# Retention's splits behind its chains, a third score ahead, squares by halves, the row behind retention in another buffer, and the second chunk one norm tile later

## The chip, the cores and the metric

The kernel runs on one core of a Trainium2 chip. The metric is the device time of one execution in microseconds (us), the median of several runs; lower is better. TensorE is called PE in the profile, its weight loads PEld, VectorE DVE, ScalarE ACT, GpSimd POOL, SyncE SP.

## What is computed

Two layers (DEPTH 2) of a diffusion trunk with D_MODEL 1024 over 512 latent tokens and 256 context tokens, all in float32:

```python
h = modulate(rms_norm(x, g_mix[l]), mod[:, :, 0], mod[:, :, 1])
y, yc = token_mixer(h, hc, ...)        # retention, latent attention, grouped attention, gates, w_out
x = x + mod[:, :, 2] * y
h2 = modulate(rms_norm(x, g_ffn[l]), mod[:, :, 3], mod[:, :, 4])
x = x + mod[:, :, 5] * swiglu(h2, w_ffn_in[l], w_ffn_out[l])
```

The context stream `xc` goes through the same steps in the first layer only; in the second it gives keys and values alone. `mod` is `silu(c) @ w_mod + b_mod`. The part that matters most here is retention, four heads with keys of 128 and values of 256 channels. Per head, with q and k rotated (rope), a score is a product of k and q times a decay that falls with the distance of the tokens; the output is the sum of scores times values:

```python
scores = jnp.einsum('bnihd,bnjhd->bnhij', qc, kc) * decay
inner = jnp.einsum('bnhij,bnjhe->bnihe', scores, vc)
y = rms_norm(y).reshape(B, T, RET_W)
return (jax.nn.silu(g.astype(jnp.float32)) * y).astype(g.dtype)
```

The kernel computes the recurrence between chunks as one masked product over all tokens, with both directions' decays in one table.

## The kernel before

**Layout.** Channels lie on the 128 partitions, tokens on the free axis: 768 of them (`TOK`), latent 512 first, in layer 0; in layer 1 queries and outputs have 512 (`LAT`). A float32 product is made of three fast ones: each operand is split into a rounded part (ACT writes it, `wh`, `hh`, `qh`, `pth`, `yh`) and a rest (DVE or POOL subtracts it, `wl`, `hl`, `ql`, `ptl`, `yl`), and `three` (L1435 is its matmul) multiplies high with high, high with low, low with high.

**Weights.** All weights come in one stream of chunks of 128 x 1024. SP loads chunk after chunk into two slots of `raw`, each when the slot's last rest is written (L423 to L425). `split(at, k)` exists twice: ACT's (L431) waits for the chunk and for the product that last used the slot and writes `wh`; DVE's (L910) then writes `wl`. `project` on PE waits for `wl` and counts `product` when it is done. Every engine works its own list of instructions in order; semaphores alone tie them together. The lists are written by hand.

**Retention** (kind `ret`): for each head PE projects q (slot 0), transposes the values from `vraw` (which ACT loads a head ahead), projects k and the gate g, and then makes 8 (layer 0) or 6 (layer 1) units: a score of 128 x 512 (or 256) into one of three PSUM banks, the product with `dec` on DVE into `prob`, the rounded part on ACT into `pth`, the rest on POOL into `ptl`, and six matmuls of values on PE. ACT and DVE prepare q and k in between (copy, rope, rounded part, rest) and split the coming weights: split(2) is g's weight, split(3) the next head's q, split(4) the next head's k. At the end of a head ACT squares both halves of the output (`y_sq`), PE sums them over the channels with `ones`, ACT takes the root (`v_std`), DVE the reciprocal, and the output is scaled, gated and split into `yh`, `yl`.

**Merge** (kind `merge`) multiplies a branch's output with its output matrix, eight chunks in four turns of two, and adds them gated to `xz`. In layer 0 each merge also computes eight columns' worth of modulation: ACT loads a row of `w_mod` (`mod_load`), PE multiplies it (`mod_row`, L1548) and folds four partial sums (`mod_fold`, L1562), DVE adds the bias (L1056, `m_add`). `rows_of` gives the two buffers of the rows: `mraw`, which shares its bytes with `dec`, and a part of `prob`. The merge behind retention has `begun` 0; those behind the attentions have 6 tiles done already.

**Two chunks at once.** `pair_tile` multiplies one normalised tile of 128 channels with the chunks in both slots while the norm makes the next tile. It is used in the kernel's start, at layer 1's entry and at the start of both feed-forward parts.

## Time and profile before

| | us |
|---|---|
| median of 3 runs | 3473.76 |
| lowest, highest | 3471.82, 3473.92 |
| the profiled execution | 3469.6 |
| its span | 3467.4 |

The mean granted clock of TensorE over the span is 0.973 of full speed. The span counts from the first instruction of the program to the last; 2.2 us of the profiled execution lie outside it. A row of the timeline gives the start, how long the group of merged instructions lasted, engine, line, operation, tiles (written <- read), their count, and in brackets the idle time of the engine before it and what ended it. Ends of matmuls are modelled and overlap the start of the next.

### The profile page before, as it was taken

Reading aid. Unit: us, or ns where it says so; the run is one execution under the profiler, and the core shown is the slowest. Engines: PE = TensorE matmul, PEld = TensorE weight load, DVE = VectorE, ACT = ScalarE, POOL = GpSimd, SP = SyncE. Lnnn points to the kernel's source line nnn. Section 1 sums busy time; section 2 is a strip of 40 time slices with the busy share of each in tenths; the row PEclk is TensorE's granted clock in tenths of the full one; section 3 lists DMA queues with packets and bytes.
Section 4 is the critical chain, followed back from the end, with each engine's and each line's share of the span. In section 5 each row is a group of like instructions: output and inputs, shape, how many; then the busy total and the mean of one; then the engine's idle time right before and its main releaser. Section 6 shows DMA issues by size and latency. Waiting matters only on the chain.

```text
span 3467.4 us, 49699 instructions
## 1 busy us (share of the span) xinstructions
PE 3218.3 (93%) x18760; PEld 2733.4 (79%) x18760; DVE 1507.6 (43%) x2047; ACT 1241.1 (36%) x1777; POOL 391.3 (11%) x304
## 2 busy tenths in 40 slices
PE   6999999999998989999999988999999988799998
PEld 5788888899887777788888867887788776678886
DVE  5555523444335533422222355553455455443334
ACT  3344432444433432321211234444355533432222
POOL 0011100111102201010100101111011101010001
PEclk9999999999999999899999999999999999989999
DMA  4221132111231244123132332222222232323222
GB/s 183 74 74 67 67 122 81 62 59 61 89 129 56 67 128 139 56 80 126 62 126 85 128 117 87 75 79 88 83 70 70 94 109 67 112 79 97 95 95 101
DMA packets 100921, 315.17 MB, mean 91 GB/s; under 512 B 11088, under 2 KB 21456, under 8 KB 100816
## 3 DMA queue, kind: packets, MB, share of 16 engines
q1 hardware_dynamic: 55872, 202.40, 17.8%
q10 hardware_dynamic: 44944, 111.32, 9.7%
q8 instruction: 72, 1.18, 0.1%
q14 instruction: 33, 0.27, 0.0%
HBM read 283.79 MB, written 29.88 MB: 90 GB/s over the span
## 4 chain that ended last, share of the span: by engine, by line
PE 48%; issue 6%; DVE 3%; ACT 2%; POOL 1%; DMA 0%; ACTq 0%; DVEq 0%; POOLq 0%
PE ps L1435 45%; PE ps L1521 1%; PE ps L1548 1%; POOL ptl L1417 1%; DVE wl L913 1%; ACT wh L439 1%; DVE tmp L923 0%; DVE hl L1088 0%; PE ps L1562 0%; DVE tmp L1079 0%; ACT prob L490 0%; PE ps L1491 0%; DMA xz<-xspill 0%; PE ps L1459 0%; ACTq L672 0%
## 5 line engine op out<-in xcount | busy, mean ns | idle before, releaser
L1435 PE MATMUL ps<-hh,wh 128*128 128x512 f32 x2768 | 832.5, 361 | 41.3 <-DVE wl L913 17.6
L1435 PE MATMUL ps<-hh,wl 128*128 128x512 f32 x2768 | 813.3, 354 | 0.0
L1435 PE MATMUL ps<-hl,wh 128*128 128x512 f32 x2768 | 813.0, 354 | 0.0
L913 DVE TENSOR_TENSOR wl<-raw,wh 128x1024 fp32r<-128x1024 f32 x364 | 484.2, 1331 | 541.2 <-ACT wh L439 512.9
L1435 PEld LDWEIGHTS ps<-hh,wh 128*128 128x128 f32 x2768 | 454.8, 191 | 123.0 <-issue 40.4
L1435 PEld LDWEIGHTS ps<-hh,wl 128*128 128x128 f32 x2768 | 453.0, 190 | 75.2
L1435 PEld LDWEIGHTS ps<-hl,wh 128*128 128x128 f32 x2768 | 453.8, 190 | 73.7 <-issue 0.7
L439 ACT ACTIVATE wh<-raw 128x1024 fp32r<-128x1024 f32 x364 | 383.2, 1054 | 222.3 <-PE ps L1435 186.6
L1435 PE MATMUL ps<-yh,wh 128*128 128x512 f32 (+1 forms) x1296 | 408.3, 369 | 30.4 <-DVE wl L913 18.9
L1435 PE MATMUL ps<-yl,wh 128*128 128x512 f32 (+1 forms) x1296 | 395.7, 360 | 0.0
L1435 PE MATMUL ps<-yh,wl 128*128 128x512 f32 (+1 forms) x1296 | 395.6, 360 | 0.0
L1370 POOL TENSOR_TENSOR prob<-prob,ri 128x768 f32<-128x768 f32 x160 | 208.3, 1303 | 1448.6 <-DVE ri L953 1448.6
L1435 PEld LDWEIGHTS ps<-yh,wh 128*128 128x128 f32 x1296 | 216.1, 191 | 83.0 <-issue 36.3
L944 DVE TENSOR_REDUCE mx<-ps 128x1 f32<-128x768 f32 x160 | 135.9, 849 | 308.8 <-PE ps L1435 308.8
L1435 PEld LDWEIGHTS ps<-yh,wl 128*128 128x128 f32 x1296 | 216.5, 191 | 37.6
L1435 PEld LDWEIGHTS ps<-yl,wh 128*128 128x128 f32 x1296 | 216.4, 191 | 36.5 <-issue 0.2
L480 ACT ACTIVATE pth<-ps 128x768 fp32r<-128x768 f32 x160 | 116.1, 726 | 308.4 <-PE ps L1521 308.3
L1435 PE MATMUL ps<-pth,vh 128*128 128x256 f32 (+1 forms) x528 | 167.8, 318 | 34.6 <-POOL ptl L1417 24.0
L1424 POOL TENSOR_TENSOR yl<-prob,yh 128x768 f32 (+1 forms) x44 | 69.1, 1570 | 845.7 <-ACT yh L892 845.7
L1435 PE MATMUL ps<-ptl,vh 128*128 128x256 f32 (+1 forms) x528 | 164.2, 311 | 0.0
L1435 PE MATMUL ps<-pth,vl 128*128 128x256 f32 (+1 forms) x528 | 164.1, 311 | 0.0
L959 DVE TENSOR_TENSOR ptl<-ps,pth 128x768 fp32r<-128x768 f32 x160 | 135.2, 845 | 58.7 <-ACT pth L480 58.6
(190 smaller groups left out, 3423.4 us busy)
## 6 DMA issues: line engine op xcount, KB each, us to landing
raw<-in_stream SPq DMA_DIRECT2D x364, 512.0 KB, 3.5
mraw<-in_wmod ACTq DMA_DIRECT2D x40, 512.0 KB, 3.5
prob<-in_wmod ACTq DMA_DIRECT2D x40, 512.0 KB, 3.5
gspill<-prob ACTq DMA_DIRECT2D x32, 384.0 KB, 2.3
tmp<-gspill ACTq DMA_DIRECT2D x24, 384.0 KB, 3.2
early_y<-in_wmod SPq DMA_DIRECT2D x12, 512.0 KB, 14.1
vraw<-gspill ACTq DMA_DIRECT2D x16, 384.0 KB, 3.9
dec<-in_dec ACTq DMA_DIRECT2D x8, 768.0 KB, 4.3
```

Of the source, the lines that this page charges most:

```text
L439: act.activation(wh[:, s, :], raw[:, s, :], ACT.Copy).then_inc(sem("w_hi"), 1)
L480: act.activation(pth[:, 0:st, (m % 2) * P:(m % 2) * P + P], ps[:, TRANS:TRANS + st * P].rearrange("p (s q) -> p s q", q=P), ACT.Copy).then ...
L913: dve.tensor_tensor(wl[:, s, :], raw[:, s, :], wh[:, s, :].bitcast(F32), ALU.subtract).then_inc(sem("w_lo"), 1)
L944: dve.tensor_reduce(mx[:, n:n + 1], ps[:, s0:s0 + w], AX.X, ALU.max).then_inc(sem("s_max"), 1)
L959: dve.tensor_tensor(ptl[:, 0:st, cols], ps[:, TRANS:TRANS + st * P].rearrange("p (s q) -> p s q", q=P), pth[:, 0:st, cols].bitcast(F32), A ...
L1370: pool.tensor_tensor(prob[:, c.prob(m), 0:w], prob[:, c.prob(m), 0:w], ri[:, col:col + 1].to_broadcast([P, w]), ALU.mult).then_inc(sem("s_ ...
L1417: pool.tensor_tensor(ptl_f[:, cols], prob[:, u % 3, 0:w], pth_f[:, cols].bitcast(F32), ALU.subtract).then_inc(sem("rs_lo"), 1)
L1424: pool.tensor_tensor(yl[:, bass.ds(2 * i + k, 1), 0:nt], prob[:, k:k + 1, 0:nt], yh[:, bass.ds(2 * i + k, 1), 0:nt].bitcast(F32), ALU.subt ...
L1435: ins = pe.matmul(out, lhs[w], rhs[x](cols), start=start and n == 0, stop=stop and n == 2)
L1521: ins = pe.transpose(ps[:, TRANS + s * P:TRANS + (s + 1) * P], prob[:, c.prob(m), s * P:(s + 1) * P], ident[:, :])
L1548: return pe.matmul(ps[r0:r0 + STRIP, col:col + P], csil[:, kt, :], x, start=kt < NSTRIP, stop=kt >= KT - NSTRIP)
```

## The change

Eight edits, all in the order of work and in one buffer:

- ACT's split(4) and the Silu of the gate's other half move from ahead of the units to behind the third rounding; DVE's split(3) moves from ahead of k's rope to behind it, and its split(4) behind the fourth decay product.
- PE issues three scores ahead instead of two.
- A new semaphore `y_half` tells ACT that the first half of the output is complete; the first square waits for it alone, and PE sums each half as soon as it is squared.
- The wait for `m_add` in `ret` moves behind the q projection, in `gqa_in` behind the first two projections.
- The merge behind retention takes its even rows from `vraw` instead of `mraw`, and ACT asks for the first row in the last head, behind the transposes of the values.
- PE waits for `v_std` before that merge's first `mod_row`, since the row's sums share a bank with retention's sums.
- `pair_tile` multiplies the second chunk one tile behind the first; the last call does both remaining tiles.

```diff
@@ plan
-             "y_sq": 2, "v_full": 2, "v_hi": 2, "v_lo": 2}, ROPED, ROPED, VALUES)
+             "y_sq": 2, "y_half": 1, "v_full": 2, "v_hi": 2, "v_lo": 2}, ROPED, ROPED, VALUES)
-        if ph["kind"].endswith("_last"):
+        if ph["kind"].endswith("_last") or ph["kind"] == "ret":
             ph["merge"] = after
@@ rows_of
-            return mraw[:, :], prob_f[:, x0:x0 + CH]
+            return vraw_f[:, 0:CH] if ph["kind"] == "merge" and not ph["begun"] else mraw[:, :], prob_f[:, x0:x0 + CH]
@@ ACT, merge
-                    if ph["nmod"]:
+                    if ph["nmod"] and ph["begun"]:
                         mod_load(ph, 0, ph["j0"])
@@ ACT, ret
                         if not last:
                             load_values(8 * i + (ph["g0"] + 4 * h + 4))
+                        elif ph["merge"]["nmod"]:
+                            mod_load(ph["merge"], 0, ph["merge"]["j0"])
...
                         act.activation(tmp[:, 1, 0:nt], pair(0)[:, 0:nt], ACT.Silu).then_inc(sem("free0"), 1)
-                        if not last:
-                            split(t, 4)
-                        act.wait_ge(sem("rg_in"), t.v("rg_in", 1) * 16)
-                        act.activation(tmp[:, 2, 0:nt], tmp[:, 2, 0:nt], ACT.Silu)
...
                             act.activation(pth_f[:, (u % 3) * LAT:(u % 3) * LAT + w], prob[:, u % 3, 0:w],
                                            ACT.Copy).then_inc(sem("rs_hi"), 1)
-                        act.wait_ge(sem("rs_used"), t.v("rs_used", units))
+                            if u == 2:
+                                act.wait_ge(sem("rg_in"), t.v("rg_in", 1) * 16)
+                                act.activation(tmp[:, 2, 0:nt], tmp[:, 2, 0:nt], ACT.Silu)
+                                if not last:
+                                    split(t, 4)
                         for e in range(2):
+                            if e == 0:
+                                act.wait_ge(sem("y_half"), t.v("y_half", 1))
+                            else:
+                                act.wait_ge(sem("rs_used"), t.v("rs_used", units))
@@ DVE, ret
-                        split(t, 3)
                         roped(t, (1, 1), 1, 1, 1, kh, kl, 0, TOK)
-                        if not last:
-                            split(t, 4)
+                        split(t, 3)
...
                                               dec[:, d0:d0 + w], ALU.mult).then_inc(sem("rs_sd"), 1)
+                            if u == 3 and not last:
+                                split(t, 4)
@@ PE, pair_tile
-                for slot in range(2):
+                for slot, g in ((0, kt), (1, kt - 1)) + (((1, kt),) if kt == KT - 1 else ()):
+                    if g < 0:
+                        continue
@@ PE, gqa_in
-                    pe.wait_ge(sem("m_add"), at.v("m_add"))
...
                         pe.wait_ge(sem("free0"), at.v("free0", j + 1))
+                        if j == 0:
+                            pe.wait_ge(sem("m_add"), at.v("m_add"))
@@ PE, merge
                                 elif ph["nmod"]:
+                                    if late and not k + r:
+                                        pe.wait_ge(sem("v_std"), at.v("v_std"))
                                     mod_fold(t, k) if r else mod_row(t, k, ph)
@@ PE, ret
-                    pe.wait_ge(sem("m_add"), at.v("m_add"))
...
                         pe.wait_ge(sem("v_std"), t.v("v_std"))
+                        pe.wait_ge(sem("m_add"), at.v("m_add"))
...
                         score(1)
+                        score(2)
...
-                            if u + 2 < units:
-                                score(u + 2)
+                            if u + 3 < units:
+                                score(u + 3)
...
+                                if e == 0 and u == units - 1:
+                                    ins.then_inc(sem("y_half"), 1)
                             ins.then_inc(sem("rs_used"), 1)
-                        pe.wait_ge(sem("y_sq"), t.v("y_sq", 2))
-                        for r0, r1 in ranges(nt):
-                            for e, x in enumerate((tmp[:, 0, r0:r1], prob[:, 2, r0:r1])):
-                                ins = pe.matmul(pair(AUX)[:, r0:r1], ones[:, :], x, start=e == 0, stop=e == 1)
+                        for e, x in enumerate((tmp[:, 0, :], prob[:, 2, :])):
+                            pe.wait_ge(sem("y_sq"), t.v("y_sq", e + 1))
+                            for r0, r1 in ranges(nt):
+                                ins = pe.matmul(pair(AUX)[:, r0:r1], ones[:, :], x[:, r0:r1], start=e == 0, stop=e == 1)
```

## Rows read from the trace of the kernel before

**Rows 1.** The page: busy time and share of the span by engine.

```profile
PE 3218.3 (93%) x18760; PEld 2733.4 (79%) x18760; DVE 1507.6 (43%) x2047; ACT 1241.1 (36%) x1777; POOL 391.3 (11%) x304
```

**Rows 2.** PE's waits, 1014 to 1231 us: releaser, total us, times, longest.

```profile
PE ps L1435 <- POOL ptl L1417: 12.5, 4, 3.7
PE ps L1819 <- ACT prob L822: 6.4, 4, 1.6
```

**Rows 3.** PE's waits, 2796 to 2975 us, layer 1's retention.

```profile
PE ps L1435 <- POOL ptl L1417: 11.4, 4, 3.3
PE ps L1435 <- DVE kl L933: 9.6, 4, 2.4
PE ps L1819 <- ACT prob L822: 4.7, 4, 1.2
```

**Rows 4.** Timeline, layer 0: first head's sums, second head's start of the units.

```profile
1065.04 1.12 PE L1819 MATMUL ps<-tmp,ones 128*128 128x512 f32 x2 [1.60 <-ACT prob L822]
...
1096.31 1.23 DVE L913 TENSOR_TENSOR wl<-raw,wh 128x1024 fp32r<-128x1024 f32 x1 [2.48 <-ACT wh L439]
1098.88 3.73 POOL L1417 TENSOR_TENSOR ptl<-prob,pth 128x512 fp32r<-128x512 f32 x3 [36.54 <-ACT pth L818]
1100.20 0.80 PE L1435 MATMUL ps<-pth,vh 128*128 128x512 f32 x1 [3.67 <-POOL ptl L1417]
```

**Rows 5.** Timeline, layer 0, last head: first product of the values.

```profile
1200.19 0.50 PE L1435 MATMUL ps<-pth,vh 128*128 128x512 f32 x1 [1.50 <-POOL ptl L1417]
```

**Rows 6.** Windows: length, busy us of PE, PEld, DVE, ACT, POOL; PEclk, DMA share, GB/s.

```profile
1100.20:1103.60 3.40, 3.40 (x8) 2.73 (x9) 0.00 (x0) 0.00 (x0) 2.41 (x2) 0.50 0.08 34
1200.20:1203.60 3.40, 3.40 (x15) 2.83 (x16) 0.69 (x1) 0.32 (x1) 2.42 (x2) 1.00 0.00 0
...
1015.40:1018.80 3.40, 3.35 (x11) 2.90 (x12) 0.97 (x1) 0.00 (x0) 0.00 (x0) 0.57 0.87 310
1231.30:1236.80 5.50, 5.49 (x30) 4.40 (x31) 1.03 (x1) 2.08 (x3) 0.00 (x0) 0.50 0.80 270
1424.50:1427.90 3.40, 3.40 (x13) 2.92 (x12) 1.96 (x1) 1.41 (x2) 1.82 (x1) 0.50 0.44 145
```

**Rows 7.** Timeline, layer 1, second head: k's copy, split(3), scores, values.

```profile
2851.68 0.81 ACT L456 ACTIVATE tmp<-ps 128x768 f32<-128x768 f32 x1 [2.09 <-PE ps L1435]
2853.47 1.23 DVE L913 TENSOR_TENSOR wl<-raw,wh 128x1024 fp32r<-128x1024 f32 x1 [1.42 <-ACT wh L439]
2859.52 0.50 PE L1435 MATMUL ps<-qh,kh 128*128 128x512 f32 x1 [2.43 <-DVE kl L933]
2865.18 0.80 PE L1435 MATMUL ps<-pth,vh 128*128 128x512 f32 x1 [3.33 <-POOL ptl L1417]
```

**Rows 8.** Timeline: first projections of `gqa_in` and of retention in layer 0.

```profile
548.29 0.61 PE L1435 MATMUL ps<-hh,wh 128*128 128x512 f32 x2 [1.18 <-DVE mods L1056]
1015.45 1.00 PE L1435 MATMUL ps<-hh,wh 128*128 128x512 f32 x2 [2.82 <-DVE mods L1056]
```

**Rows 9.** Timeline, layer 0: last head's rests, first row and fold of the merge.

```profile
1225.22 1.83 DVE L1283 TENSOR_TENSOR yl<-prob,yh 128x768 fp32r<-128x768 f32 x2
1231.31 1.08 PE L1548 MATMUL ps<-mraw,csil 128*32 128x128 f32 x16 [9.82 <-DMA mraw<-in_wmod]
1233.14 0.26 ACT L598 ACTIVATE tmp<-ps 128x128 f32<-128x128 f32 x1
1238.64 0.28 PE L1562 MATMUL ps<-sel,tmp 128*128 128x2 f32 x2
```

**Rows 10.** Timeline: the kernel's start, and the third chunk of both feed-forward parts.

```profile
39.38 0.16 DVE L1119 TENSOR_TENSOR mods<-ps,bmod 128x4 f32<-128x4 f32 x1 [2.31 <-PE ps L1667]
1423.36 0.59 PE L1435 MATMUL ps<-hh,wh 128*128 128x512 f32 x2 [2.15 <-DVE wl L913]
3100.56 0.77 PE L1435 MATMUL ps<-hh,wh 128*128 128x512 f32 x1 [2.30 <-DVE wl L913]
```

**Rows 11.** One line's view, L913: count, ns minimum/median/maximum, first and last start.

```profile
L913 DVE TENSOR_TENSOR wl<-raw,wh x364: 1215/1226/2156, 18.2 to 3447.2; 128x1024 fp32r<-128x1024 f32 x182
```

More of the change, by code:

```diff
@@ L332, in build @@
         prob_f = prob[:, :, :].rearrange("p a b -> p (a b)")
+        vraw_f = vraw[:, :, :].rearrange("p a b -> p (a b)")
         def rows_of(ph):
             x0 = 2 * TOK if ph["kind"] == "merge" else 0
-            return mraw[:, :], prob_f[:, x0:x0 + CH]
+            return vraw_f[:, 0:CH] if ph["kind"] == "merge" and not ph["begun"] else mraw[:, :], prob_f[:, x0:x0 + CH]
         keys, queries = ((kh, kl), (k2h, k2l)), ((qh, ql), (q2h, q2l))
@@ L1252, in turn @@
                                           ALU.subtract).then_inc(sem("vt_lo"), 1)
+                        roped(t, (1, 1), 1, 1, 1, kh, kl, 0, TOK)
                         split(t, 3)
-                        roped(t, (1, 1), 1, 1, 1, kh, kl, 0, TOK)
-                        if not last:
-                            split(t, 4)
                         units = 8 if nt > LAT else 6
@@ L1464, in pair_tile @@
                 pe.wait_ge(sem("n_lo"), at.v("n_lo", kt + 1 + since))
-                for slot in range(2):
+                for slot, g in ((0, kt), (1, kt - 1)) + (((1, kt),) if kt == KT - 1 else ()):
+                    if g < 0:
+                        continue
                     s = at.slot(slot)
                     outs = [(pair(slot)[:, r0:r1], (r0, r1)) for r0, r1 in ranges(nt)]
-                    ins = three(outs, [w[:, s, whole(kt)] for w in (wh, wl)],
-                                [lambda c, x=x: x(kt, c) for x in H], kt == 0, kt == KT - 1)
-                    if kt == KT - 1:
+                    ins = three(outs, [w[:, s, whole(g)] for w in (wh, wl)],
+                                [lambda c, x=x: x(g, c) for x in H], g == 0, g == KT - 1)
+                    if g == KT - 1:
                         ins.then_inc(sem("product"), 1)
```

## The prediction

> **What bounds the kernel now.** I read the page first: TensorE is busy for 93% of the span and no other engine for half of it [rows 1], so time comes back only where TensorE waits or runs slowly. Then I listed TensorE's waits over the two retention stages and looked at each in the timeline. In layer 0 the four heads hold 12.5 us of waits for POOL's `ptl` and 6.4 us for ACT's squares [rows 2]; in layer 1 they hold 11.4 us for `ptl`, 9.6 us for DVE's `kl` and 4.7 us for the squares [rows 3]. Around them lie single waits: 1.18 and 2.82 us for the last sum of the modulation (`mods`) [rows 8], and 9.82 us for a row of w_mod, the longest behind the kernel's first [rows 9]. Last comes the clock: in 3.4 us TensorE starts 15 matmuls of 512 columns at full clock (0.227 us each) and 8 at half of it [rows 6]. So a long wait is paid again behind its end: 15 matmuls' worth of time gives 8, and 3.4 us at half clock cost up to 1.7 us, 1.6 with the matmuls counted (8 x 0.2).
>
> **Splits behind the chains.** TensorE's first values product needs score, decay product (DVE), rounding (ACT) and rest (POOL). In the heads before the last one DVE makes the split of the next k weight first, 1.23 us from 1096.31 [rows 4], behind ACT's part of it; the first product of the values starts at 1100.20 after 3.67 us idle [rows 4]. The last head has no such split: there the wait is 1.50 us, with the same three scores before it [rows 5]. That is what the change makes of the others: 3.67 - 1.50 = 2.17 us a head in layer 0. The clock stands at 0.50 behind the 3.67 us and at 1.00 behind the 1.50 us [rows 6], so 1.6 us more. The split itself is not free: on ACT the gate's Silu (0.8 us for a pass over 768 columns [rows 7]) and the split (1024 columns, so 1.1 us) now stand between the third and fourth rounding, on DVE 1.23 us between the fourth and fifth decay product. Behind the first values product TensorE needs 9 x 0.227 = 2.05 us a unit (one score, two values), the chain of a unit only what POOL needs, 3.73 us for three, 1.25 each [rows 4]; stepping the chain through with the durations of this case I find each later rest ready 0.4 to 2 us before TensorE asks. I take nothing for it. Bounds: nothing, and 1 us a head if that cover is short.
>
> **Splits and the shared queue.** The L913 rows last 1.22 us in the middle and up to 2.16 us [rows 11]; the split now runs beside POOL's `ptl`, where a long one is possible. It would use up 0.9 us of a cover of 0.4 to 2 us. The Trainium skill ("SBUF — State Buffer", section "Who interferes with whom") says that a VectorE tensor_tensor with both inputs in SBUF and a GpSimd instruction that reads SBUF exclude one another for a whole instruction. By that rule each of six heads could give back up to 1 us, 6 us in all; the rows' spread agrees with it, their middle does not show it. The sum goes without it.
>
> **Third score.** It was already issued before the first wait; now the fourth is too, 3 x 0.227 = 0.68 us of TensorE work that fills part of the 1.50 us left. Its bank is freed by the first decay product, which ends before the third score does. 0.68 us a head, eight heads.
>
> **k's rope ahead of split(3).** In layer 1 the scores wait 2.43 us for `kl` [rows 7]. DVE idled 1.42 us until ACT's part of split(3), then split for 1.23 us until 2854.7, then began k's rope [rows 7]; k's copy had been there since 2852.5 (2851.68 + 0.81) [rows 7]. The rope can start then: 2.1 us earlier, with 0.3 us of wait left. All four heads of layer 1 show this wait (9.6 us in four) [rows 3]. In layer 0 nothing waits for `kl` and I count nothing. split(3) then ends about when the first score does; it may hold the first decay product by 0.1 us. It is wanted a whole head later, and the reload of its raw buffer, which SyncE's queue issues behind it, with it.
>
> **Layer 1's chain** shows 3.33 us before the values product [rows 7]; three such and one of 1.48 make the 11.4 us [rows 3]. So 3.33 - 1.48 = 1.85 us less 0.1 for split(3), plus 1.6 us of clock, in three heads.
>
> **Squares by halves.** The first square starts when the last unit's first half is done, 3 matmuls of 256 columns (0.36 us) earlier in layer 0 and 3 of 512 (0.68 us) in layer 1, and the sums over it start at once; the second square (0.8 us) lies beside them, as even the first two matmuls of the sums take 1.12 us [rows 4]. The wait of 1.60 us (6.4 in four) [rows 2] falls to about 0.5, that of 1.18 (4.7 in four) [rows 3] to 0.1: 1.1 us a head, eight heads.
>
> **Heads, summed.** Layer 0: 3 x (2.17 + 1.6 + 0.68 + 1.1) + (0.68 + 1.1) = 18.4 us. Layer 1: 3 x (2.1 + 1.75 + 1.6 + 0.68 + 1.1) + (2.1 - 0.1 + 0.68 + 1.1) = 21.7 + 3.8 = 25.5 us. Behind a head's sums the order of root, reciprocal, products and `yl` is as before, so nothing of this is taken back before the next head's transposes.
>
> **m_add later.** The two waits of 1.18 and 2.82 us [rows 8] stood before a projection that doesn't need them; their semaphore comes 1.2 and 2.9 us after TensorE is ready, and the projections take 8 us or more. Behind the 2.82 us the clock is 0.57 on the mean for 3.4 us [rows 6], so up to 1.6 us more; I take 1.5. 1.2 + 2.8 + 1.5 = 5.5 us. The k weight's split isn't wanted until 9 us later.
>
> **Row behind retention.** Now the row's transfer is issued only after the last `yl` (1225.22 to 1227.05), since `mraw` shares its bytes with `dec`; TensorE idles from 1221.5 to 1231.31 [rows 9] and runs at 0.50 until 1236.8 [rows 6]. With the row in `vraw`, loaded a head earlier, its product runs at 1221.5, two tiles follow, and the last two wait for `yl` until 1227.1. They end at about 1228.4. What is late next is the fold: it needs ACT's copy of the row's sums, which stands on ACT behind the wait for `yl`, a split, two table loads and a Sigmoid and starts at 1233.14 [rows 9]. The fold thus moves from 1238.64 [rows 9] to 1233.4: 5.2 us. TensorE idles 4.7 us before it, so the tiles behind run at half clock for one stretch, 1.6 us back. I take 3.6; bounds 2.0 (two stretches) and 5.2 (none). The added wait for v_std holds nothing: the root is over three tiles before.
>
> **Second chunk a norm later.** The first chunk's product now ends a tile earlier against the same total (a tile: 3 x (512 + 256) columns, 1.0 us, or 0.7 us at 512). Where TensorE works without idling from the first norm on and then waits for the next weight's `wl` (2.15 us at 1423.36, 2.30 us at 3100.56) [rows 10], the wait shrinks by that: 1.0 and 0.7 us. Behind the first of them the clock was 0.50 [rows 6], behind the second a matmul took 0.77 us [rows 10]; with 1.1 and 1.6 us left, which elsewhere did not lower it, 1.6 us each. In the kernel's start one tile fewer stands before the third fold, where DVE idles 2.31 us [rows 10]; behind that both engines are without idle, so I take half, 1.1 (0 to 2). At layer 1's entry the norm sets the pace and ACT's split covers the later tile: 0. Sum 1.0 + 0.7 + 3.2 + 1.1 = 6.0 us.
>
> **Sum.** 18.4 + 25.5 + 5.5 + 3.6 + 6.0 = 59.0 us. The profiled execution took 3469.6 us (span 3467.4); it would be 3410.6. The median of the runs is 4.2 us above it: 3473.8 - 59.0 = 3414.8 us.
>
> **Rivals.** (1) The clock is not given back: shorter waits, but more of them in a row (about 1 us before the values, 0.5 before the sums) still lower it in the heads and at the norms. Against it speaks the last head's 1.00 behind 1.50 us [rows 6]; for it, that half clock stood behind a wait of only 2.15 us. The sum loses 6 x 1.6 + 1.5 + 3.2 = 14.3 us: 3429 us. (2) The cover inside the chain is short, 1 to 2 us a head in six heads, and the fold behind retention stays where it was: 6 to 12 + 3.6 us, 3424 to 3430 us. (3) The change doesn't do what it says: split(4) in the middle of the chain makes the fourth unit late by what it took off the first, so only k's rope, the squares and the single waits remain: 59.0 - 3 x (2.17 + 1.75) - 6 x 1.6 - 8 x 0.68 = 32 us, 3442 us. (4) Slower: ACT's split(4) waits on raw data or on the g product while the roundings 4 to 8 stand behind it in ACT's order, and DVE's part holds decay products 5 to 8; TensorE idles once a head in mid-chain. It needs more than 59 us over six heads, about 10 us a head, to end above 3474 us; at 12 us a head it ends at 3487. From a wait of 2 us on it costs anything. Against it: the raw chunk is asked for behind the split of the g weight, a whole product (8 us) before the scores, and the g product is over when they start.
>
> **How the numbers follow.** Forecast 58%: 3408 to 3421. Rivals 1 and 2 together 25%, rival 3 8%, rival 4 3%, more gain than summed (clock kept behind retention too, start in full) 6%, to 3405. The range is 3404 to 3434. About 0.2% (7 us) is what a measurement can tell from no change: faster 0.95, same 0.02, slower 0.03.
>
> **What would show it.** Right: waits for `ptl` of about 1 us in all eight heads, none over 0.5 us for `kl`, under 0.6 us for squares, full clock in retention, no wait for `mods`, and a wait for ACT's `tmp` of over 3 us at the first fold behind retention instead of one for `mraw`. Wrong: a wait for `ptl` in mid-chain, half clock behind waits near 1 us, a longer wait before layer 1's first norm tiles.

## The result, and the profile after

The changed kernel takes 3413.4 us (median of four runs, 3408.3 to 3424.5) beside 3473.8 us before (four runs, 3471.8 to 3476.9) on the same chip: ratio 0.9831, 95% interval 0.9817 to 0.9845, so faster by 1.7%. Forecast were 3414.8 us and a ratio of 0.983. Measured again beside other runs of the kernel before it took 3413.7 us, ratio 0.9827 (0.9814 to 0.9841). One execution of e1 below took 3879 us at a mean granted clock of 0.78, where every other one lies at 0.97 or above; it is left out there. The profiled execution took 3408.35 us, span 3406.2: 61.2 us less than the span before.

The page after, span and busy time by engine, to be read against [rows 1]:

```profile
span 3406.2 us, 49718 instructions
PE 3200.3 (94%) x18760; PEld 2716.6 (80%) x18760; DVE 1512.8 (44%) x2047; ACT 1241.8 (36%) x1777; POOL 397.4 (12%) x304
```

TensorE's instructions are the same in number and 18 us shorter in sum, which is clock and not work (36.1 us less at half clock, by the figures below, are 18 us of work); the other 43 us are idle time that is gone. DVE and POOL are busy for 5 and 6 us more: that is the split lying beside POOL, below.

The waits of TensorE after, layer 0's retention (1005 to 1210 us), against [rows 2] (engine, line, releaser: total us, times, longest):

```profile
PE ps L1572 <- ACT tmp L600: 4.3, 1, 4.3
PE ps L1443 <- POOL ptl L1425: 3.3, 4, 0.8
PE ps L1835 <- ACT tmp L830: 2.2, 4, 0.5
PE ps L1443 <- DVE yl L1291: 1.9, 1, 1.9
```

and layer 1's (2757 to 2915 us), against [rows 3]:

```profile
PE ps L1443 <- POOL ptl L1425: 3.2, 4, 0.8
PE ps L1443 <- DVE yl L1291: 2.2, 1, 2.2
PE ps L1443 <- DVE kl L941: 1.3, 4, 0.3
```

The 12.5 and 11.4 us for `ptl` are 3.3 and 3.2, the 9.6 us for `kl` are 1.3, the squares' 6.4 us are 2.2, and in layer 1 they left the list. The wait for a row of w_mod, 9.82 us in [rows 9], is gone, and the fold's wait for ACT's `tmp` stands in its place, as a new line.

The timeline after, TensorE: second head's first values product, the rest of the merge's first tiles, the fold, and the two third chunks of the feed-forward parts, against [rows 4], [rows 9] and [rows 10] (start, length, instruction, tiles, in brackets the idle time ahead of it and what ended it):

```profile
1080.48 0.50 PE L1443 MATMUL ps<-pth,vh 128*128 128x512 f32 x1 [0.81 <-POOL ptl L1425]
...
1195.67 0.63 PE L1443 MATMUL ps<-yh,wh 128*128 128x512 f32 x2 [1.86 <-DVE yl L1291]
...
1202.40 0.59 PE L1572 MATMUL ps<-sel,tmp 128*128 128x2 f32 x2 [4.34 <-ACT tmp L600]
...
1390.51 0.59 PE L1443 MATMUL ps<-hh,wh 128*128 128x512 f32 x2 [1.12 <-DVE wl L921]
...
3040.95 0.47 PE L1443 MATMUL ps<-hh,wh 128*128 128x512 f32 x1 [1.63 <-DVE wl L921]
```

Windows after, behind four of these, against [rows 6] (length, busy us of PE, PEld, DVE, ACT and POOL, PEclk, DMA share, GB/s):

```profile
1080.50:1083.90 3.40, 3.40 (x15) 2.78 (x16) 2.48 (x2) 2.21 (x3) 3.38 (x3) 1.00 0.00 0
1202.40:1208.30 5.90, 5.90 (x19) 5.13 (x20) 3.16 (x4) 1.74 (x2) 0.00 (x0) 0.50 0.78 263
1390.50:1393.90 3.40, 3.39 (x19) 2.98 (x20) 1.54 (x2) 1.79 (x2) 1.58 (x1) 1.00 0.50 152
3041.00:3044.40 3.40, 3.40 (x15) 2.81 (x16) 1.75 (x2) 1.58 (x2) 1.29 (x1) 1.00 0.47 154
```

In the head's units 15 matmuls now lie in 3.4 us where 8 did. Over the whole span the granted clock stands at its lower level (1.2 GHz) for 189.5 us before and 153.4 after.

**Where the 61.2 us lie**, between events that both traces have (the start of the n-th split of a weight on DVE, or the last sums of a head):

| stretch | forecast us | measured us |
|---|---|---|
| kernel's start, third fold | 1.1 | 1.7 |
| latent attention (no edit in it) | 0 | 5.0 |
| layer 0: `m_add` at the grouped attention | 1.2 | 1.0 |
| layer 0: `m_add` at retention and the four heads | 2.8 + 1.5 + 18.4 | 22.8 |
| layer 0: row and fold behind retention | 3.6 | 2.9 |
| layer 0: out projection | 0 | -1.5 |
| layer 0: feed-forward pair | 1.0 + 1.6 | 2.0 |
| pace of the two feed-forward loops | 0 | -3.9 |
| layer 1: entry | 0 | 1.7 |
| layer 1: the four heads | 25.5 | 27.1 |
| layer 1: feed-forward pair | 0.7 + 1.6 | 2.4 |
| sum | 59.0 | 61.2 |

Of the heads, one in layer 0 takes 45.5 us instead of 51.1, one in layer 1 36.7 instead of 44.3 (start of `dec`'s transfer to the next head's). A head's gain can be taken apart from its waits. In layer 0 TensorE idled 3.67 + 1.60 = 5.3 us in a head and now idles 0.81 + 0.54 = 1.35, which is 3.9 us; the 3.4 us at half clock behind the long wait are gone too, which is 1.7. In layer 1 it idled 2.43 + 3.33 + 1.18 = 6.9 us and now 0.34 + 0.81 = 1.15, so 5.8 us, and 1.7 of clock again. That makes 5.6 and 7.5 us, beside the 5.6 and 7.6 measured.

The 1.7 us at layer 1's entry belong, in all likelihood, to the change as well. The norm there is one that `pair_tile` works beside. TensorE, before and after, and what stood behind the wait:

```profile
2045.76 1.19 PE L1491 MATMUL ps<-prob,ones 128*128 128x512 f32 x1 [2.48 <-ACT prob L691]
2015.73 0.67 PE L1501 MATMUL ps<-prob,ones 128*128 128x512 f32 x1 [1.81 <-ACT prob L693]
```

```profile
2045.80:2049.20 3.40, 3.40 (x5) 1.44 (x5) 0.10 (x1) 0.00 (x0) 0.00 (x0) 0.51 0.51 152
2015.80:2019.20 3.40, 3.40 (x14) 2.21 (x15) 0.83 (x2) 0.69 (x1) 0.00 (x0) 1.00 0.47 151
```

The wait is 1.8 us in all eleven traces with the second chunk a tile later, with the clock at 1.00 behind it in every one. It is 2.5 us in the three with both chunks together (before, e6 and e8), and the clock fell behind it in two of them.

### The profile page after: what moved, and what is told of

Same layout as the page of the kernel before. It is cut to its first block, busy times and chain, and to the rows that moved or that the text cites. A ratio compares the mean times of both kernels' runs of the same rounds, so it can differ in the third digit from the quotient of the medians.

```text
span 3406.2 us, 49718 instructions
## 1 busy us (share of the span) xinstructions
PE 3200.3 (94%) x18760; PEld 2716.6 (80%) x18760; DVE 1512.8 (44%) x2047; ACT 1241.8 (36%) x1777; POOL 397.4 (12%) x304
## 3 DMA queue, kind: packets, MB, share of 16 engines
q8 instruction: 72, 1.18, 0.1%
## 4 chain that ended last, share of the span: by engine, by line
PE 52%; DVE 4%; issue 3%; ACT 2%; POOL 0%; DMA 0%; ACTq 0%; DVEq 0%; POOLq 0%
PE ps L1443 49%; PE ps L1531 1%; PE ps L1558 1%; DVE wl L921 1%; ACT wh L441 0%; POOL ptl L1425 0%; DVE tmp L931 0%; DVE hl L1096 0%; PE ps L1572 0%; DVE tmp L1087 0%; DMA xz<-xspill 0%; PE ps L1467 0%; ACT prob L492 0%; ACTq L674 0%; PE ps L1501 0%
```

## The experiments

The yardstick is the changed kernel, 3413.4 and 3413.7 us. Its own runs lie up to 16 us apart, and so do those of its variants, so a median of four decides a term of 5 us only roughly. Each experiment was therefore also read by the length of a head (first `ptl` to first `ptl`) and by the wait that it was made for. Intervals are those of the ratio to the kernel before, taken on the same chip in turns. The experiments ran on three chips, where the kernel before took 3475.1, 3474.5 and 3471.6 us; only the last one, that of e9 to e11, also timed the changed kernel. Read by the ratios instead of the medians a difference moves by up to 3 us (e3 5.9 instead of 8.8, e6 3.5 instead of 6.6, e10 5 instead of 8.0), and only e11's interval lies clear of the changed kernel's own. So the medians say which way an edit works, and its size rests on the heads and the waits.

**The splits back ahead of the chains (e1).** In retention, on ACT and DVE:

```diff
@@ ACT, ret, ahead of the units
+                        if not last:
+                            split(t, 4)
+                        act.wait_ge(sem("rg_in"), t.v("rg_in", 1) * 16)
+                        act.activation(tmp[:, 2, 0:nt], tmp[:, 2, 0:nt], ACT.Silu)
@@ in the units, u == 2
-                                act.wait_ge(sem("rg_in"), ...); Silu; split(t, 4)
@@ DVE, ret
                         split(t, 3)
+                        if not last:
+                            split(t, 4)
@@ in the units, u == 3
-                                split(t, 4)
```

> The changed kernel with split(4) and the gate's second Silu put back ahead of the units, on ACT and DVE; all else as changed. Theory A (the first values product waits for what stands ahead of the chain, and a wait near 3 us lowers the clock): in six heads the wait for ptl is 3.67 - 0.68 = 3.0 us in layer 0 and 3.33 - 0.68 = 2.7 us in layer 1 instead of 0.8, the clock behind it is 0.50, and the kernel is 6 x 2.0 + 6 x 1.6 = 21 to 22 us slower than the changed one. Theory B (the clock falls only behind 3.3 us and more): same waits, clock 1.00, 12 us slower. Theory C (split(4) costs the same in mid-chain): no difference.

Measured: 3430.2 us (three runs, 3424.3 to 3439.8), ratio 0.9874 (0.9841 to 0.9907), 16.6 us over the yardstick. A head of layer 0 takes 49.2 us twice and then 45.4, in layer 1 38.5; by the splits of the weights the two retention stages lost 8.3 and 6.8 us against the changed kernel, 15.1 together. Timeline of e1, TensorE, second head, and windows behind the waits of two heads of layer 0 and two of layer 1:

```profile
1095.78 0.50 PE L1442 MATMUL ps<-qh,kh 128*128 128x512 f32 x1 [1.64 <-DVE prob L1273]
...
1097.80 0.80 PE L1442 MATMUL ps<-pth,vh 128*128 128x512 f32 x1 [1.05 <-POOL ptl L1424]
```

```profile
1097.80:1101.20 3.40, 3.40 (x9) 2.72 (x10) 0.69 (x1) 0.38 (x1) 2.42 (x2) 0.59 0.09 35
1147.00:1150.40 3.40, 3.40 (x15) 2.83 (x16) 1.38 (x2) 0.63 (x1) 3.38 (x3) 1.00 0.04 14
2840.50:2843.90 3.40, 3.38 (x15) 2.81 (x16) 1.38 (x2) 0.63 (x1) 3.38 (x3) 1.00 0.06 23
2879.10:2882.50 3.40, 3.40 (x8) 2.72 (x9) 0.69 (x1) 0.39 (x1) 2.41 (x2) 0.52 0.08 30
```

The wait is there as worked out, 2.7 us (forecast 3.0), in two pieces, since the fourth score now stops for the bank that the first decay product frees. What fell short of the 21 to 22 us is the clock. It is low behind this wait in three heads of six, where I had put it at six: 3 x 1.6 = 4.8 us less, which leads to 16.7. The rival that the splits cost nothing is out by the heads; that of 12 us is not excluded by the median's interval, but the heads' 15.1 speak against it.

**split(3) ahead of k's rope (e2)**, the order before, on DVE:

```diff
-                        roped(t, (1, 1), 1, 1, 1, kh, kl, 0, TOK)
                         split(t, 3)
+                        roped(t, (1, 1), 1, 1, 1, kh, kl, 0, TOK)
```

> The changed kernel with DVE's split(3) put back ahead of k's rope. Theory A: in layer 1 the wait for kl is 2.4 us again instead of 0.3 in four heads, layer 0 shows none, 8.4 us slower than the changed kernel. Theory B: the wait before the values becomes shorter by what split(3) no longer holds the first decay product, so under 8 us. Both expect layer 0's heads unchanged; if they are longer, kl mattered there too.

Measured: 3424.5 us (3417.7 to 3426.7), ratio 0.9855 (0.9837 to 0.9872), 10.9 us over. Layer 0's heads are unchanged (45.5), layer 1's take 39.0 instead of 36.7, 9.2 us in four. Waits of e2, layer 1, and a window behind the second head's wait for `kl`:

```profile
PE ps L1443 <- DVE kl L941: 9.6, 4, 2.4
PE ps L1443 <- POOL ptl L1425: 1.6, 2, 0.8
```

```profile
2821.90:2825.30 3.40, 3.28 (x9) 2.63 (x10) 1.45 (x3) 1.66 (x4) 0.63 (x1) 0.61 0.04 15
```

The wait for `kl` is that of [rows 3] to the tenth, and 8.3 us of it (9.6 - 1.3) are the term. The waits for `ptl` shrank by 1.6 us in turn (3.2 to 1.6), so by difference 2.5 us are clock: behind the 2.4 us it was low in two heads of four.

**Two scores ahead (e3).**

```diff
                         score(1)
-                        score(2)
...
-                            if u + 3 < units:
-                                score(u + 3)
+                            if u + 2 < units:
+                                score(u + 2)
```

> The changed kernel with two scores ahead of the values instead of three (the third is issued ahead of the first wait either way, the fourth not). Theory A: the wait for ptl is 1.5 us instead of 0.8 in all eight heads, clock unchanged, 8 x 0.68 = 5.4 us slower than the changed kernel. Theory B (the fourth score's place matters in mid-chain as well, since split(4) delays the fifth decay product): more, with new waits for ptl in mid-chain.

Measured: 3422.4 us (3415.5 to 3424.1), ratio 0.9848 (0.9832 to 0.9865), 8.8 us over; heads 0.7 us longer in layer 0 and 1.0 in layer 1, 6.8 us in eight. Waits of e3 in layer 0:

```profile
PE ps L1443 <- POOL ptl L1425: 6.0, 4, 1.5
```

The wait grows from 0.8 to 1.5 us, by one score (0.68), as said; the other 0.3 us of a head in layer 1 are in no wait. Eight waits of 1.5 us leave the clock at 1.00, as the last head's did in [rows 6].

**Squares whole (e4)**: both squares behind the last unit, the sums behind both.

```diff
-                        for e in range(2):
-                            if e == 0:
-                                act.wait_ge(sem("y_half"), t.v("y_half", 1))
-                            else:
-                                act.wait_ge(sem("rs_used"), t.v("rs_used", units))
+                        act.wait_ge(sem("rs_used"), t.v("rs_used", units))
+                        for e in range(2):
@@ PE: pe.wait_ge(sem("y_sq"), t.v("y_sq", 2)) once, ahead of all the sums
```

> The changed kernel with both squares behind the last unit and the sums behind both squares, as before. Theory A: the wait before the sums is 1.6 us instead of 0.55 in layer 0 and 1.2 instead of under 0.1 in layer 1, clock unchanged, 8 x 1.1 = 8.8 us slower than the changed kernel. Theory B: the head's tail (root, reciprocal, yl) covers part of it, since it starts later against the next projection: under 8 us. The tail is as long as before in both, so B has to show it in a shorter wait elsewhere.

Measured: 3421.4 us (3418.5 to 3430.9), ratio 0.9857 (0.9835 to 0.9880), 7.8 us over; heads 1.1 and 1.15 us longer, 9 us in eight. In layer 1 the wait of [rows 3] is back, each 1.2 us:

```profile
PE ps L1830 <- ACT prob L827: 4.7, 4, 1.2
```

**The row in `mraw` again (e5)**, loaded by the merge itself, as before the change.

```diff
@@ rows_of
-            return vraw_f[:, 0:CH] if ph["kind"] == "merge" and not ph["begun"] else mraw[:, :], prob_f[:, x0:x0 + CH]
+            return mraw[:, :], prob_f[:, x0:x0 + CH]
@@ ACT, merge
-                    if ph["nmod"] and ph["begun"]:
+                    if ph["nmod"]:
                         mod_load(ph, 0, ph["j0"])
@@ ACT, ret
-                        elif ph["merge"]["nmod"]:
-                            mod_load(ph["merge"], 0, ph["merge"]["j0"])
```

> The changed kernel with the rows of the merge behind retention in mraw again, the first asked for behind the last yl. Theory A: 9.8 us of wait for mraw instead of 1.9 for yl and 4.3 for ACT's tmp; the fold comes 5.2 us later, of which the half clock behind the changed kernel's 4.3 us gave 1.6 to 3 back: 3 us slower than the changed kernel at the merge's second turn, 3.6 by the forecast. Theory B (the changed kernel lost nothing to the clock there): 5.2 us slower.

Measured: 3416.1 us (3415.0 to 3419.4), ratio 0.9839 (0.9822 to 0.9855), 2.5 us over. The timeline of e5 shows the old wait back in full:

```profile
1204.58 1.08 PE L1556 MATMUL ps<-mraw,csil 128*32 128x128 f32 x16 [9.85 <-DMA mraw<-in_wmod]
```

Almost 10 us of waiting are worth some 3 us, because 6.2 us of other waits take their place (1.86 for `yl`, 4.34 for `tmp`) and low clock stands behind both kernels' long wait. A difference of 2.5 us is within what four runs scatter; that it is the 3.6 us of the forecast rather than the 5.2 of its upper bound rests on the events (2.9 us).

**Both chunks of a norm's pair together (e6).**

```diff
-                for slot, g in ((0, kt), (1, kt - 1)) + (((1, kt),) if kt == KT - 1 else ()):
-                    if g < 0:
-                        continue
+                for slot, g in ((0, kt), (1, kt)):
```

> The changed kernel with both chunks of pair_tile at the same tile, as before. Theory A: waits of 2.15 and 2.30 us for the third weight of the feed-forward parts instead of 1.1 and 1.6, with half clock behind each: 1.0 + 0.7 + 3.2 us; the start is 1.1 to 1.7 us later; 6 to 7 us slower than the changed kernel. Theory B (the clock behind the waits depends on where its stretch happens to lie, not on 2.15 against 1.1 us): 3 to 4 us slower, the layer 0 feed-forward showing full clock.

Measured: 3420.2 us (3413.7 to 3427.7), ratio 0.9841 (0.9822 to 0.9861), 6.6 us over. Timeline of e6, third chunks:

```profile
1402.24 0.58 PE L1443 MATMUL ps<-hh,wh 128*128 128x512 f32 x2 [2.14 <-DVE wl L921]
...
3058.73 0.77 PE L1443 MATMUL ps<-hh,wh 128*128 128x512 f32 x1 [2.30 <-DVE wl L921]
```

Both waits of [rows 10] are back (2.15 and 2.30 there), the clock is low behind both, and 1.0 and 0.7 us is what the change takes off them. At layer 1's entry the wait is 2.50 us again with low clock behind it, and the stretch 1.6 us longer: the third place where this edit works.

**m_add ahead of the first projection (e7)**, in `gqa_in` and in retention:

```diff
@@ PE, gqa_in, ahead of the projections
+                    pe.wait_ge(sem("m_add"), at.v("m_add"))
@@ PE, ret, ahead of the first turn
+                    pe.wait_ge(sem("m_add"), at.v("m_add"))
@@ and the two waits behind the projection taken out
```

> The changed kernel with both waits for m_add ahead of the first projection again. Theory A: waits of 1.2 and 2.8 us for mods, 0.57 of the clock behind the second: 5.5 us slower than the changed kernel. Theory B (the k or v side of the stage sets the pace, so an earlier q projection gains less): under 4 us.

Measured: 3419.7 us (3419.1 to 3420.2), ratio 0.9846 (0.9829 to 0.9862), 6.1 us over. Timeline of e7:

```profile
1016.01 0.74 PE L1443 MATMUL ps<-hh,wh 128*128 128x512 f32 x2 [2.82 <-DVE mods L1064]
```

**The kernel before, with the wait filled (e8).** This tries the clock by itself: eight matmuls whose result nobody reads stand in the wait before a head's first values product.

```diff
+                            if u == 0:
+                                for n in range(8):
+                                    pe.matmul(ps[:, 7 * BANK:8 * BANK], kh[:, 0:P], qh[:, 0:LAT], start=True, stop=True)
                             pe.wait_ge(sem("rs_lo"), t.v("rs_lo", u + 1))
```

> The kernel before with eight matmuls of 512 columns into an unused PSUM bank behind the third score of each head, inside the wait for the first ptl; their result is read by nobody. It tells the wait from its clock. Eight take 8 x 0.227 = 1.8 us of a wait of 3.3 to 3.7 us (in the two last heads 1.5 us: 0.3 us too long each). Theory A (idle time lowers the clock): the first values product starts when it did, the clock behind it is 1.00, the six heads gain 1.6 us each, 9 to 10 us faster than the kernel before. Theory B (the half clock has another cause, as what the first values product reads): no gain.

Measured: 3466.3 us (ten runs, 3451.5 to 3473.1) beside 3475.1 before, ratio 0.9970 (0.9954 to 0.9986), so 8.8 us less as a median. But the profiled execution, 3470.0 us, is no shorter than that of the kernel before (3469.6): layer 1's retention is 2.8 us shorter in it, and the feed-forward loops of layer 0 are 4.2 us slower (see the last section). Timeline, layer 0, second head, then windows behind that wait and behind the second head's in layer 1:

```profile
1099.74 1.75 PE L1809 MATMUL ps<-qh,kh 128*128 128x512 f32 x7
...
1103.35 0.50 PE L1435 MATMUL ps<-pth,vh 128*128 128x512 f32 x1 [1.85 <-POOL ptl L1417]
```

```profile
1103.30:1106.70 3.40, 3.35 (x10) 2.64 (x11) 0.00 (x0) 0.00 (x0) 2.47 (x2) 0.64 0.06 22
2868.00:2871.40 3.40, 3.40 (x16) 2.81 (x15) 0.69 (x1) 0.63 (x1) 2.03 (x3) 1.00 0.02 5
```

In layer 1 the rests of the wait are 1.5 us in the first and third head, with the clock at 1.00 behind them. In the second the clock fell earlier, behind the 2.4 us for `kl`, and the slowed scores and idle matmuls filled the wait to its end. A head takes 42.8 us on the mean instead of 44.3: 1.5 us for no less work, which shows that low clock behind a wait is a price of its own. In layer 0 1.85 us of idling are left, the clock is low all the same in three heads of three, and a head takes the 51.1 us of before. My theory here, that a filled wait gives the clock back everywhere, holds for half of it. How much of the 8.8 us on the median comes from the clock in the heads can't be told from one trace.

**The changed kernel again (after_again)**, with no edit.

> The changed kernel itself, timed again as the yardstick of the others. Its four runs lay 16 us apart (3408.3 to 3424.5), the granted clock with them (0.978 to 0.974). Theory A (the spread is the clock: where its stretches fall against the waits, anew in each execution): the same waits for every semaphore, other half-clock stretches, the median between 3410 and 3420. Theory B (something of the order differs): other waits.

Measured: 3413.7 us (five runs, 3407.6 to 3415.3). The waits in the heads are the same; the stretches of low clock in the latent attention lie elsewhere, 153.0 us in all beside 153.4. The latent attention takes 4.3 us longer here than in the first trace of the same kernel. So the 5.0 us that it seemed to gain are no part of the change: before, the clock was low at 83.1 and 339.1 us; after, it stood at 1.00 there. Windows before, then after, at nearly the same time (the same work lies 3 to 6 us earlier after, at 1.00 as well):

```profile
339.00:345.80 6.80, 6.80 (x34) 6.80 (x34) 1.31 (x2) 0.83 (x2) 0.19 (x1) 0.50 0.24 77
```

```profile
339.00:346.00 7.00, 6.09 (x40) 5.22 (x38) 4.02 (x7) 3.29 (x6) 0.61 (x1) 1.00 0.00 0
```

**Three more passes in mid-chain (e9)** measure the cover that hides the split: three copies of 512 columns on ACT, 1.95 us together with what lies between, ahead of split(4).

```diff
+                                for n in range(3):
+                                    act.activation(prob[:, 3, 0:LAT], qh[:, 0:LAT].bitcast(F32),
+                                                   ACT.Copy).then_inc(sem("pass"), 1)
+                                    act.wait_ge(sem("pass"), t.v("pass", n + 1))
                                 if not last:
                                     split(t, 4)
```

> The changed kernel with three useless passes of ACT over 512 columns (0.63 us each and a wait between them, some 2.1 us together) ahead of split(4), behind the gate's Silu, in every head. It measures the cover of what was moved into the chain. Theory A (forecast's stepping: later rests are ready 0.4 to 2 us before they are asked for): layer 0 shows no or hardly any wait for ptl in mid-chain, layer 1 0.5 to 1.7 us a head in three or four heads, 2 to 7 us slower than the changed kernel. Theory B (no cover): 8 x 2.1 = 17 us slower. Theory C (cover everywhere over 2 us): no difference.

Measured: 3418.1 us (3416.2 to 3420.9), ratio 0.9842 (0.9826 to 0.9857), 4.5 us over; heads 0.1 to 0.2 us longer in layer 0, 0.5 in layer 1. Timeline of e9 on ACT, and TensorE's waits in its layer 1:

```profile
2871.47 1.95 ACT L824 ACTIVATE prob<-qh 128x512 f32<-128x512 f32 x3
```

```profile
PE ps L1447 <- POOL ptl L1429: 3.2, 4, 0.8
```

ACT's two extra microseconds a head lie under TensorE's work almost whole. The 0.5 us a head in layer 1 show no new wait of over 0.3 us. The heads account for some 2 us of the 4.5; the rest is within the scatter.

**split(4) in the last head too (e10).** The last head's ACT and DVE are as free in mid-chain as the others', and the merge behind retention begins with a split of its own:

```diff
@@ ACT and DVE, ret, in the units
-                                if not last:
-                                    split(t, 4)
+                                split(t, 4)
@@ ACT and DVE, merge behind retention
+                            if begun or k:
-                            split(t, k + 1)
+                                split(t, k + 1)
```

> The changed kernel with split(4) in the last head as well, which is the second chunk of the merge behind retention; the merge's first turn leaves it out. Theory A (what is late behind retention is that split, behind the wait for v_lo): layer 1's wait of 3.2 us for wl and its half clock go (3 to 4.8 us faster than the changed kernel); in layer 0 the wait for ACT's tmp at the first fold becomes 1.1 to 2.3 us shorter, since ACT reaches the copy of the row's sums a split earlier. Together 5 to 7 us faster. Theory B (the gate's Sigmoid or its load comes next in line): under 3 us.

Measured: 3405.6 us (3400.6 to 3413.1), ratio 0.9813 (0.9795 to 0.9831), 8.0 us less. Timeline of e10 at the fold:

```profile
1205.15 0.38 PE L1580 MATMUL ps<-sel,tmp 128*128 128x2 f32 x2 [0.96 <-ACT tmp L600]
```

The fold's wait falls from 4.34 to 0.96 us, since the split stood on ACT ahead of the row's copy, and the stretch behind retention ends 5.3 us earlier against the changed kernel; in layer 1 a wait of 3.16 us for `wl` behind retention is gone with the low clock behind it, 5.1 us. One stretch of low clock is left in layer 0, behind the wait of 1.79 us for `yl`; in the changed kernel the clock stayed up behind that wait:

```profile
1200.40:1203.80 3.40, 3.40 (x11) 2.92 (x12) 0.69 (x1) 1.28 (x1) 0.00 (x0) 0.50 0.46 148
```

Some 2.9 us were lost elsewhere to the clock. I had put both at less, 1.1 to 2.3 us for the fold's wait and 3 to 4.8 us for layer 1.

**The row's copy ahead too (e11)**: e10, and ACT copies the first row's sums before it waits for the last g products.

```diff
+                    if ph["nmod"] and not ph["begun"]:
+                        mod_row(at, 0)
                     act.wait_ge(sem("g_out"), at.v("g_out") * 16)
...
-                            if ph["nmod"]:
+                            if ph["nmod"] and (begun or k):
                                 mod_row(t, k)
```

> As e10, and ACT copies the first row's sums ahead of its wait for v_lo instead of behind gate, split and Sigmoid. Theory A: the first fold no longer waits (4.3 us in the changed kernel), so the half clock behind it goes too; with e10's gain in layer 1 it is 8 to 10 us faster than the changed kernel, 3403 to 3407 us on the median. Theory B (another wait takes its place in the second chunk: the product of DVE's gate or the slot): under 5 us.

Measured: 3399.2 us (five runs, 3393.8 to 3406.7), ratio 0.9790 (0.9775 to 0.9805), 14.4 us below the changed kernel, the fastest of all. TensorE's waits of e11 behind layer 0's retention (1195 to 1220 us), and the window that stood at 0.50:

```profile
PE ps L1453 <- DVE yl L1301: 1.8, 1, 1.8
```

```profile
1201.60:1208.40 6.80, 6.78 (x40) 5.74 (x40) 2.74 (x3) 3.19 (x3) 0.00 (x0) 1.00 0.65 214
```

No wait for the fold is left and no low clock behind retention: 40 matmuls lie in 6.8 us, where after the change 19 did in 5.9. Against e10 this place gives 2.0 us more, and only 0.96 of them are the fold's wait. The rest is the low clock that stood in e10 behind the wait for `yl`; e11 has the same wait, 1.8 us, with full clock behind it, so that part is not shown to be the edit's (in the eleven traces with this wait the clock fell behind it in two). 12.4 us of the 14.4 lie behind the two retention stages (7.3 and 5.1). The other 2 are within the scatter.

## Why the prediction was right

The forecast was within 1.4 us of both medians, with one compensation in it. By its steps:

- **Splits behind the chains, third score, squares, clock in the heads.** Right in each size: in layer 0 a head became 5.6 us shorter (2.17 + 1.6 + 0.68 + 1.1 = 5.55), in layer 1 7.6 (7.2). The waits came out at 0.8 us, 0.3 for `kl`, 0.5 and about nothing for the squares, all as said. Undone one by one, splits, rope, score and squares give back 15.1, 9.2, 6.8 and 9 us by the heads, 40 in all; the heads gained 45.6 (22.8 + 27.1 less 4.3 for `m_add`). By the trace the clock's share of the gain is six stretches of 1.7 us, 10 in all. Undone one by one the edits bring back fewer: three in e1, two in e2, none in e3 and e4, some 7.5 us. Another 1.6 us is e2's, whose longer wait for `kl` shortens the one behind it. These two make some 4 of the 5.5 us that are missing; the rest is open.
- **The cover inside the chain.** Taken at nothing, with 0.4 to 2 us to spare; right in its effect. TensorE has no wait over 0.3 us in mid-chain, and e9 adds 1.95 us on ACT for 0.1 to 0.5 us a head. So rival 2's short cover is out, and with it rivals 3 and 4, which needed TensorE held up in mid-chain.
- **The split beside POOL.** I left it out of the sum and it happens, in all six heads. The timeline after, DVE and POOL, layer 1, second head (the first row merges four of POOL's instructions):

```profile
2820.73 6.03 POOL L1425 TENSOR_TENSOR ptl<-prob,pth 128x512 fp32r<-128x512 f32 x4 [27.58 <-ACT pth L818]
...
2823.48 2.13 DVE L921 TENSOR_TENSOR wl<-raw,wh 128x1024 fp32r<-128x1024 f32 x1 [0.67 <-ACT wh L441]
```

  The split takes 2.13 us instead of 1.23, and of POOL's rests, 1.3 us each, one takes 2.22:

```profile
2824.55 2.22 POOL L1425 TENSOR_TENSOR ptl<-prob,pth 128x512 fp32r<-128x512 f32 x1
```

  POOL's third rest ran until 2824.52, and the split, begun at 2823.48, ended 1.09 us behind it; POOL's fourth, begun at 2824.55, ended 1.15 us behind the split. Each was longer by what the other still had to do, 0.9 us each time. That fits the rule of the Trainium skill ("SBUF — State Buffer", "Who interferes with whom") that was weighed in the prediction: the two exclude one another for a whole instruction. It costs TensorE nothing here, since 0.9 us fit the cover, so the sum without it was the right one.
- **Rival 1, the clock not given back.** Out in the heads: behind waits of 0.8 us it stood at 1.00 in every head of this kernel, its repetition and seven experiments. But how I put it for all heads alike was too simple, as e1 and e8 show (next section but one).
- **m_add later.** 5.5 us forecast, 6.1 by e7, and in the trace after no wait for `mods` at either place.
- **Row behind retention.** 3.6 us forecast, 2.9 by the events, 2.5 by e5. The fold came 5.7 us earlier (5.2 forecast). The term that was mis-sized is the clock behind it: 6.8 us at 0.50 gave back 2.8 us, not 1.6, two stretches rather than one, inside the bound I had kept. It falls either way: behind the same 4.3 us of wait, five traces (after, its repetition, e6, e7, e9) show 6.8 us of low clock and three (e1, e2, e3) 3.4.
- **Second chunk a norm later.** The waits fell by 1.0 and 0.7 us to 1.12 and 1.63, and the clock stayed up: 4.4 us of 4.9, and 6.6 by e6. The kernel's start gave 1.7 of a possible 2, where I took 1.1. The 0 for layer 1's entry was wrong. The norm sets the pace there, as said: in e8, where the clock stayed up, the stretch is as long as after the change. But the wait for the norm fell from 2.5 to 1.8 us and the low clock behind it went, 1.7 us in this trace and 1.6 back in e6. It stood there in two traces of three, so some 1 us was to be taken.
- **What no step held.** The latent attention gained 5.0 us by clock stretches that fell elsewhere, the feed-forward loops lost 3.9 by a slower pace, and the out projection 1.5, which the repetition doesn't show. These cancel to -0.4 us; that the profiled sum came within 2.2 us of the span is partly this luck, with the 1.7 us at layer 1's entry on top.

The largest wait that I said would come next, for ACT's `tmp` at the fold, was the one worth going after: e10 and e11 took it away, and with it the wait for `wl` behind layer 1's retention, and gained 14.4 us, a quarter of the change's own gain, with two moves.

## What to carry to other kernels

Order the first links of a chain (score, product, rounding, rest) ahead of anything that is wanted later, and look for its new place where the consumer has a unit's worth of work per link; extra passes of 2 us in such a place cost here 0.1 to 0.5 us a head. Price a wait on TensorE at its length plus the low clock behind it, and when a wait is removed ask at once what stands second on the engine that now releases it: here a split ahead of a copy. A term of 5 us in 3400 is better read from the length of a loop's turn than from the medians of four runs.

## What the runs showed of the hardware that I had not expected

**Low clock behind a wait is not a matter of its length alone.** In the heads: behind 0.8 us never (nine executions of eight kernels), behind 1.5 us never (eight heads of e3), behind 1.6 us for the squares never (four heads each of before, e4 and e8), behind 1.85 us filled ahead by matmuls in three of three (e8), behind 2.4 us for `kl` in two of four (e2), two of four (e8) and none of four (before), behind 2.7 us in two pieces in three of six (e1), behind 3.3 to 3.7 us in six of six (before). Outside the heads: behind the 1.8 us for `yl` after layer 0's retention in two traces of eleven (e4, e10), behind the 2.15 and 2.30 us ahead of the third chunks in six of six (before, e6, e8), behind the 1.1 and 1.6 us that the change left there in none of 22. At layer 1's entry it fell behind 2.5 us in two of three and behind 1.8 us in none of eleven. So between about 1.8 and 3 us it falls either way, in 15 of the 27 cases above 2 us here. What decides in a single case the runs don't show.

**Two paces at full clock.** A feed-forward loop without a wait runs at either of two paces, for a whole loop at a time. Windows of one such loop before, and of two after:

```profile
1460.00:1493.00 33.00, 33.00 (x193) 28.87 (x192) 8.65 (x6) 6.85 (x8) 3.70 (x2) 1.00 0.19 64
```

```profile
1470.00:1503.00 33.00, 33.00 (x189) 28.66 (x188) 7.72 (x7) 7.10 (x8) 3.70 (x2) 1.00 0.20 64
1650.00:1683.00 33.00, 33.00 (x192) 28.84 (x191) 8.38 (x6) 7.10 (x8) 3.70 (x2) 1.00 0.20 64
```

TensorE is busy throughout and the granted clock is 1.00 in all three, yet 193 and 192 matmuls lie in the window where 189 do in the second: four chunks of weights take 33.3 or 33.9 us. Before, all three loops of layer 0 ran at 33.3; after, two ran at 33.9; e6 ran all three at 33.9; the repetition of the changed kernel ran the first at 33.3. The same code does both, so it is a matter of the execution, worth some 2 us a loop. Its cause stays open. Layer 1's loops, with 512 tokens, show one pace alone, 21.8 us for four chunks in all fourteen traces. Together with low-clock stretches that fall elsewhere from one execution to the next, the pace is the likely source of the 16 us between runs of one kernel; that was not tried. The clock can account for up to 10 to 14 of the 16 us: 153.4 us at half clock cost the run of 3408 us up to 77 us, and a mean granted clock of 0.974 means 87 to 91 in the run of 3424 us. But it alone does not order the runs: in the repetition one of 3414.5 us had 0.980 and one of 3407.6 us 0.978.
